# Feed-forward of a two-model kernel: which PSUM banks the first unit leaves, when a down step waits for its banks, and where weight splits and modulation steps stand

## The reference, cut to what matters

```
def _swiglu(h, w_ffn_in, w_ffn_out):
    gate, up = jnp.split(h @ w_ffn_in, 2, axis=-1)
    return (jax.nn.silu(gate) * up) @ w_ffn_out
...
def conv_ffn(h, w_up, conv_w, conv_b, w_down):
    u = h @ w_up
    ...
    for j in range(CONV_W):
        acc = acc + up[:, j:j + L] * conv_w[j]
    a, g = jnp.split(acc, 2, axis=-1)
    return (jax.nn.silu(g) * a) @ w_down
...
m_lat = [m[:, None, :] for m in jnp.split(jax.nn.silu(c) @ ada_w[l] + ada_b[l], 6, axis=-1)]
```

## Time and profile before

| | |
|---|---|
| median of three runs | 2430.82 us |
| the profiled execution | 2431.32 us, span 2429.5 us |
| outside the span | 1.8 us |
| mean granted TensorE clock | 0.988 of 2.4 GHz |
| PE busy | 2324.1 us, 96% of the span |
| DVE busy | 1549.6 us, 64% |
| ACT busy | 949.2 us, 39% |
| GpSimd (POOL) busy | 349.5 us, 14% |
| feed-forward of block 0 | from about 427 to 798 us |
| feed-forward of block 1 | from about 1222 to 1800 us |
| feed-forward of block 2 | from about 2048 us to the end |

### The profile page before, as it was taken

How to read it: one execution, slowest core, us unless ns; L and a number is a source line. 1 busy time by engine, 2 the same in 40 slices (tenths; PEclk the granted TensorE clock), 3 DMA queues, 4 the chain that set the end, 5 groups by cost and what they waited for, 6 DMA issues and landing times.

```text
span 2429.5 us, 33136 instructions
## 1 busy us (share of the span) xinstructions
PE 2324.1 (96%) x13146; PEld 1885.6 (78%) x13146; DVE 1549.6 (64%) x2465; ACT 949.2 (39%) x1768; POOL 349.5 (14%) x455
## 2 busy tenths in 40 slices
PE   6999899999999899999999999999999999999998
PEld 3876567888887788777878888888877778888886
DVE  3648686566767652566879885656474767765457
ACT  4426464322222421566342232332352774423333
POOL 0110100000022210101000313223112120101131
PEclk8999999999999999999999999999998999999999
DMA  6330024744544312110422333234122103432321
GB/s 263 118 108 25 19 88 163 250 170 156 167 136 156 110 56 80 68 62 9 166 66 94 131 122 110 96 108 139 44 79 78 37 14 143 150 111 87 104 87 70
DMA packets 79178, 257.58 MB, mean 106 GB/s; under 512 B 5680, under 2 KB 10416, under 8 KB 70576
## 3 DMA queue, kind: packets, MB, share of 16 engines
q1 hardware_dynamic: 65024, 205.01, 24.5%
q0 software_dynamic: 12704, 46.14, 5.5%
q10 hardware_dynamic: 1296, 4.30, 0.4%
HBM read 246.00 MB, written 9.44 MB: 105 GB/s over the span
## 4 chain that ended last, share of the span: by engine, by line
PE 81%; DVE 9%; ACT 3%; issue 3%; DMA 2%; POOL 1%; SPq 1%; POOLq 0%; DVEq 0%; ACTq 0%
PE PS L1288 11%; PE PS L1289 11%; PE PS L1290 11%; PE PS L1359 5%; PE PS L1360 5%; PE PS L1361 5%; PE PS L1165 4%; PE PS L1204 3%; PE PS L1184 3%; PE PS L996 3%; PE PS L999 3%; PE PS L997 3%; PE PS L1053 1%; PE PS L1257 1%; PE PS L1260 1%
## 5 line engine op out<-in xcount | busy, mean ns | idle before, releaser
L1288 PE MATMUL PS<-HH,WH 128*128 128x512 f32 (+1 forms) x1088 | 420.8, 387 | 9.2 <-DVE TMP L2578 4.6
L1289 PE MATMUL PS<-HL,WH 128*128 128x512 f32 (+1 forms) x1088 | 417.2, 383 | 0.0
L1290 PE MATMUL PS<-HH,WL 128*128 128x512 f32 (+1 forms) x1088 | 417.1, 383 | 0.0
L2771 ACT ACTIVATE WH<-STG 128x1024 fp32r<-128x1024 f32 (+1 forms) x202 | 196.7, 1022 | 272.6 <-PE PS L1361 236.1
L2365 DVE TENSOR_TENSOR WL<-STG,WH 128x1024 fp32r<-128x1024 f32 (+1 forms) x202 | 241.8, 1238 | 37.0 <-ACT WH L2771 36.9
L1288 PEld LDWEIGHTS PS<-HH,WH 128*128 128x128 f32 x1088 | 204.6, 188 | 53.7 <-issue 5.7
L1359 PE MATMUL PS<-WH,AH 128*128 128x512 f32 x600 | 235.8, 393 | 7.4 <-DVE WL L2365 3.4
L1898 DVE SCALAR_TENSOR_TENSOR ACC<-ADAW,CS,ACC 128x1024 f32<-128x1024 f32 x168 | 225.4, 1377 | 21.8 <-PE PS L999 14.4
L1290 PEld LDWEIGHTS PS<-HH,WL 128*128 128x128 f32 x1088 | 204.6, 188 | 40.1
L1289 PEld LDWEIGHTS PS<-HL,WH 128*128 128x128 f32 x1088 | 204.7, 188 | 39.9 <-issue 1.0
L1360 PE MATMUL PS<-WL,AH 128*128 128x512 f32 x600 | 234.5, 391 | 0.0
(11 more groups left out here) (273 smaller groups left out, 4451.6 us busy)
## 6 DMA issues: line engine op xcount, KB each, us to landing
STG<-in_w_up SPq DMA_DIRECT2D x66, 1024.0 KB, 6.3
ADAW<-in_w_ada SPq DMA_DIRECT2D x96, 512.0 KB, 3.8
STG<-in_w_down SPq DMA_DIRECT2D x20, 1024.0 KB, 5.1
ADAW<-in_w_ada POOLq DMA_DIRECT2D x32, 512.0 KB, 4.0
STG<-in_w_ffn_out SPq DMA_DIRECT2D x10, 1024.0 KB, 6.3
STG<-in_ev_w_in SPq DMA_DIRECT2D x8, 1024.0 KB, 5.1
STG<-in_w_in SPq DMA_DIRECT2D x6, 1024.0 KB, 7.0
spill<-X POOLq DMA_DIRECT2D x10, 512.0 KB, 5.1
```

Of the source, the lines that this page charges most:

```text
L1288: e.matmul(out, h_, hh, start=c == 0, stop=False)
L1289: e.matmul(out, h_, hl, start=False, stop=False)
L1290: return e.matmul(out, l_, hh, start=False, stop=c == 7)
L2771: return e.activation(dst, src, ACT.Copy)
```

## The change

The line numbers of the changed kernel are 12 to 26 higher than those of the kernel before; L1371 there is L1359 here, L1920 is L1898, L2387 is L2365, L2487 is L2465, L2593 is L2569, L2615 is L2589, L2797 is L2771, L3197 is L3171, L3207 is L3181.

Behind the first unit of each block's feed-forward the rotation skips two banks. A down step still names all its banks at its start, but waits for each one only at the first matmul that writes it. The weights of `pi` 28 in blocks 0 and 2 are split inside unit `pi` 26 on ACT and DVE. And the modulation steps of `pi` 26 in block 0 and of `pi` 7 in block 1 stand earlier on DVE.

```diff
+def split_inside(L, pi):
+
+    return apart(L, pi) or (L != 1 and pi == 28)
...
-    def take(key):
+    def claim(key):
         b = rot["set"][rot["n"] % len(rot["set"])]
         rot["n"] += 1
         k.bank[key] = b
+        return b
+
+    def bank_free(b):
         for s in freed[b]:
             w.wait_ge(*s)
+
+    def take(key):
+        b = claim(key)
+        bank_free(b)
         return b
...
                 if pi == 0:
                     first_up(wh, wl)
+                    rot["n"] += 2
...
-                    bs = {tt: take(("down", L, g, h, tt)) for _, tts in groups for tt in tts}
+                    bs = {tt: claim(("down", L, g, h, tt)) for _, tts in groups for tt in tts}
...
                     for tt in LAT:
+                        if i == 0:
+                            bank_free(bs[tt])
                         down(pi, 0, tt, bs[tt], c, [i], us)
...
                     for tt in tts:
+                        if c == 0 and (gi or not len(ahead)):
+                            bank_free(bs[tt])
                         m = down(pi, gi, tt, bs[tt], c, range(0 if gi else len(ahead), n), us)
...
-    return L == 1 and pi in (0, 6, 7, 10, 11, 12)
+    return L == 1 and pi in (0, 6, 10, 11, 12)
+
+
+def step_ahead(L, pi):
+
+    return (L, pi) in ((0, 26), (1, 7))
...
                     if L == 0:
                         z = y[0]
+                        if step_ahead(L, pi):
+                            step(bg, 2)
                         w.wait_ge(*k.ac_y((L, pi, gi)))
...
                         for j in range(2):
                             ch = (L - 1) * 132 + j * 22 + q[2]
+                            if step_ahead(L, pi) and (gi, j) == (0, 1):
+                                step(bg)
                             w.wait_ge(*k.ac_y((L, pi, gi, j)))
...
-                    if step_by_group(L, pi):
+                    if step_by_group(L, pi) or ((L, gi) == (1, 0) and step_ahead(L, pi)):
                         step(bg)
...
-                    if apart(L, pi + 2):
+                    if split_inside(L, pi + 2):
                         split_up(L, pi + 2)
...
-            if not step_by_group(L, pi):
+            if not step_by_group(L, pi) and not step_ahead(L, pi):
                 step(bg, ffn_steps(L, pi))
```

More of the change, by code:

```diff
@@ L2553, in ffn @@
             if pi + 1 < len(plan):
-                if not apart(L, pi + 1):
+                if not split_inside(L, pi + 1):
                     split_up(L, pi + 1)
```

## The result

The changed kernel takes 2413.6 us (median of 4 runs, 2413.27 to 2414.33), the kernel before 2432.51 in its four (2429.23 to 2435.26). The ratio is 0.993, 95% interval 0.9918 to 0.9942: faster by 0.6 to 0.8%. The forecast was 2415 with a range of 2409 to about 2423. The profiled execution took 2414.33 us with a span of 2412.5; it is 17.0 us under the profiled one of before, where the prediction had 16.5.

What follows compares the result with a forecast made beforehand. PE, busy for 96% of the span, was taken as the bound. 6.84 - 0.3 + 4.52 + 1.5 + 3.91 = 16.5 us off the profiled 2431.3 gave 2414.8, forecast 2415, range 2409 to about 2423.

Steps and rivals of the forecast that it cites:

- Rotation skip: Stops at the second unit of each block (443.44, 1243.41, 2066.11) go: 6.84 us, less 0.3 us in block 2.
- give-back: In block 2 at `pi` 3, PE arrives earlier against WL, so 0 to 0.7 us come back; 0.3 us taken.
- A stop's own cost: Each of eight PE stops costs 0.26 us beyond its bracket: 0.16 us from bracket start, about 0.1 us slow first matmul.
- Banks one by one: Stops at 1374.25, 1453.64 and 1471.24 go, as PE waits only for the bank each tile needs: 4.52 us.
- The 85 waits: Down matmuls that newly carry a wait: taken as costing nothing, bounds 0 and 0.1 us each, 8.5 us.
- The half clock: Half-clock stretch behind the stop at 1374.25 goes with that stop, at 2 in 3: 1.5 us, bounds 0 and 1.7.
- Unit 26: Stops for WL of `pi` 28 in blocks 0 and 2 (744.83, 2357.64) go through split and moved steps: 3.91 us.
- `pi` 7: Block 1: a moved modulation step lets LOW start some 2 to 3 us earlier, with nobody waiting: worth 0.
- the part taken back: Rival: the next late thing, such as WL in the first units, takes part of the gain: 2421 us, chance 0.2.
- Banks late at their first tile: Rival: each late bank is the first tile's and unit 26's stop passes on; only the skip works: 2424.5, chance 0.09.
- a price on waits: Rival: each of the 85 waits opens a gap, at 0.25 us 21 us: 2436 us, slower, chance 0.04.
- moving on: Clock rival: half-clock stretch stays or moves to another place of short PE work: 2416.5 or 2419.5 us, chance 0.12.

Runs made afterwards that it cites:

- skip alone: The kernel before with only the rotation skip behind each block's first feed-forward unit added: 2423.42 us, ratio 0.9976.
- 1412 more of the kind: The changed kernel with a wait for a long past semaphore value added on every first matmul of a triple: 2416.35 us, ratio 0.9933 to before.
- the split alone: The kernel before with only the weights of `pi` 28 split inside unit 26, modulation steps left where they stood: 2428.35 us, ratio 0.9992.
- the banks alone: The kernel before with only the banks of a down step awaited one by one: 2423.34 us, ratio 0.9973.
- Alone, these steps: The kernel before with only the modulation steps of unit 26 in block 0 and `pi` 7 in block 1 moved forward: 2423.5 us, ratio 0.9975.

## Why the prediction was right, step by step

- **Rotation skip:** forecast 6.84 - 0.3 = 6.54 us, measured 1.54 + 2.44 + 2.54 - 0.35 = 6.17 (skip alone 6.17 too: 1.50 + 2.44 + 2.57 - 0.34). The mechanism is right, and the size of the give-back; but it comes at `pi` 4, and I had worked it out for `pi` 3, where PE meets no wait. Its reason, WL's slack eaten by the earlier PE, holds one unit on.
- **A stop's own cost:** booked at 0.26 us for each of eight, 2.08 in all. The eight gains are 14.45 us for 13.19 of brackets (the stretch behind the 1374 us stop taken out at 1.64), so 1.26 in all, 0.16 each: 0.2 to 0.3 at four of them (745, 1243, 1471 and 2357 us), 0 to 0.1 at the other four, where shorter matmuls stand ahead and the first long one is slow even without the stop (0.47 us at 438.52 and 2050.02, 0.50 at 1364.91 and 1441.44, in the kernel after). This term is nearly the whole of the 0.7 us by which 16.47 is over 15.74.
- **Banks one by one:** forecast 4.52, and 1.5 for the clock; measured 5.66 with the clock, of it 1.64 the clock's. Right, with the stops 0.5 us over by their own cost. The 85 waits cost nothing that shows, by 1412 more of the kind.
- **The half clock:** the sum is right and the reason only in part. I took the stretch to belong to the stop at 1374 us. The skip alone and the split alone have that stop without it, and the banks alone remove it there and get one at 1242 us. Counted over profiles it goes with having these stops at all: six of seven profiles that have some of the eight have one stretch, the seven without the eight have none. All three profiles of before had exactly one to lose, so 1.5 us was rightly booked; that it stood behind a stop of this change in the first was chance, as in the second it stood behind the fold. The Trainium skill's rule on swings between bursts that cycle PSUM banks (TensorE: Matmul & The Clock Gate, "A second HAM failure mode: psum-queue depth-cycling") asks for small idles; the changed kernel cycles the banks as much, has none of the eight idles, and its clock holds at 1.00 there. The trace agrees in so far as the stretches stood behind idles and not where banks merely cycled. For an edit that removes some of the stops the credit is open: three of the four parts alone still had one stretch; only with all eight stops gone was it away each time.
- **Unit 26:** forecast 3.91, measured 2.55 + 1.36 = 3.91. The landings were 5.6 us for the weights and not 4.9, and 0.26 us of waiting for ADAW, both inside the room that was worked out (WL of `pi` 28 is 2.5 us ahead of PE, forecast 2.3). I didn't see that the split is needed in block 2 alone, nor that without the moved steps WL of `pi` 29 would be late. I had said that this WL "stays as it was against PE"; it takes 3.51 us, not 4.23, and is done at 742.25, 0.6 us before PE comes to `pi` 29 at 742.88, where in before it was still at work then (until 751.82, PE at 750.37).
- **`pi` 7:** no gain of its own in the full change, as said, but LOW came 0.85 us sooner and not 2 to 3, since AL waits for ACT's AH. Alone, these steps do gain 0.84 us at the 1374 us stop.
- **The rivals:** the part taken back was 0.35 us in the full change; it is real where one part is done alone (the split, 1.4 of 3.9 us). Banks late at their first tile, and a price on waits, are refuted. Of the stretches forecast as "moving on", one did stand at 1147 us in the profile after, 1.64 us, where the profile of before had none. Eleven of the fourteen profiles have one near there, the second of before at 1155 us among them, while the third has none; so it needs no change to come, though no run rules out that the change makes it likelier.
- **Luck, and what is open:** the profiled gain of 17.0 us is so near to 16.5 because 1.24 us from unedited stages, the sum of half-clock stretches that fell here or there, more than cover the 0.7 us that were booked too high. The runs differ by 17 to 19 us in the median and the feed-forwards by 15.0 to 15.8. The 1 to 4 us left are inside what the unedited stages vary between runs (423.8 to 430.1 us ahead of the first feed-forward for one kernel, 3.2 of these 6.3 us at the half-clock stretch at 280 us); no run here shows whether the change has a part in it.

## What to carry to other kernels

Where one engine is busy for 96% of the span, list its brackets, and for each ask only whether the awaited work could stand earlier on its engine or be waited for later; price a stop at its bracket plus 0 to 0.3 us. Look at the next weight or buffer behind each stop: a part alone may return half of its gain there, as the split did. Compare programs with the same instruction order stage by stage, by instruction number: gains of 1 us are plain in this, while five runs don't resolve them. Look at the granted clock at the places that differ before you put a difference down to an edit.

## What the runs showed of the hardware that I had not expected

- A matmul's wait for a semaphore that is long past costs under 0.3 ns (1412 added, feed-forwards 1287.85 us against 1287.80 and 1288.19).
- The half-clock stretches inside the three feed-forwards, six in fourteen profiles, begin within 2 us behind a stop of 1.66 to 2.28 us, at a different one from run to run of one kernel, and cost 1.5 to 1.8 us each.
- One kernel's stages outside the feed-forwards differ by up to 6.3 us between executions, while its feed-forwards repeat to 0.1 us where no stretch stands. A half-clock stretch at 280 us, there in six of fourteen profiles and in each kind of kernel, makes 1.7 to 3.4 us of it.
